# Where the stationary blocks of the expert matmuls begin, modulo 256 bytes

## The reference

```python
D_MODEL = 1024; N_EXPERTS = 32; TOP_K = 4; D_FF = D_MODEL
h = x + mix @ w_out
hn = rmsnorm(h, g_ffn_norm)
logits = (hn @ w_router).astype(jnp.float32) + b_router
top_v, top_e = lax.top_k(logits, TOP_K)
gates = jax.nn.softmax(top_v, axis=-1)
# for every block of rows that belongs to expert e:
h = xb @ w_gate_up[e] + b_gate_up[e]
gate = jnp.minimum(h[:, 0::2], SWIGLU_LIMIT)
up = jnp.clip(h[:, 1::2], -SWIGLU_LIMIT, SWIGLU_LIMIT)
glu = gate * jax.nn.sigmoid(gate * SWIGLU_ALPHA)
out = ((up + 1.0) * glu) @ w_down[e] + b_down[e]
y = h + sum over the 4 experts of gate * out
```

## Time and profile before

| | |
|---|---|
| median of 3 runs | 1380.27 us (1379.94 to 1383.11) |
| the profiled execution, its own time | 1378.44 us |
| its span, first to last instruction | 1376.7 us |
| PE busy | 1347.8 us, 98% of the span |
| DVE busy | 1208.2 us, 88% |
| ACT busy | 1090.7 us, 79% |
| mean granted TensorE clock | 0.993 of full speed |
| HBM | 340 GB/s over the span |

### The profile page before, as it was taken

One profiled execution on the slowest core, in us unless ns is written; L12 is line 12 of the kernel. 1 busy time (PEld: TensorE's weight loads), 2 busy tenths in 40 slices (PEclk: granted clock), 3 DMA queues, 4 the chain that ended last, 5 costly groups with the idle time before them and its releaser, 6 DMA issues.

```text
span 1376.7 us, 19701 instructions
## 1 busy us (share of the span) xinstructions
PE 1347.8 (98%) x6762; PEld 997.0 (72%) x6762; DVE 1208.2 (88%) x1092; ACT 1090.7 (79%) x1149; POOL 993.9 (72%) x431
## 2 busy tenths in 40 slices
PE   8999999999999999999999999999999999999995
PEld 5988655667777777777777777777777777777773
DVE  5466555899999999999999999999999999999996
ACT  5354413788889888888888888888888888888885
POOL 2122212266699999999999898898888888989843
PEclk9999998999999999999999999999999999999998
DMA  9521271999999999999999999999999999999984
GB/s 354 192 67 67 94 275 70 354 395 371 368 351 376 369 378 383 386 383 388 372 388 395 368 390 371 385 374 383 381 391 375 383 386 379 385 377 386 382 313 151
DMA packets 51802, 458.99 MB, mean 333 GB/s; under 512 B 11449, under 2 KB 15515, under 8 KB 26121
## 3 DMA queue, kind: packets, MB, share of 16 engines
q1 hardware_dynamic: 40089, 438.33, 81.1%
q0 software_dynamic: 10000, 18.19, 6.0%
q10 hardware_dynamic: 1648, 1.65, 0.4%
HBM read 446.62 MB, written 22.08 MB: 340 GB/s over the span
## 4 chain that ended last, share of the span: by engine, by line
PE 70%; DVE 6%; POOL 3%; issue 2%; DMA 1%; ACT 1%; POOLq 0%; ACTq 0%; DVEq 0%
PE psum L2376 22%; PE psum L2375 22%; PE psum L2374 22%; DVE low L1693 4%; PE psum L2358 1%; PE psum L2369 1%; DMA area<-hn_tbl,idx_i 1%; POOL brow L671 1%; POOL slot_tbl L724 1%; PE psum L1913 1%; POOL small L813 0%; DVE area L1775 0%; DVE area L1778 0%; DVE area L1768 0%; DVE area_r L1757 0%
## 5 line engine op out<-in xcount | busy, mean ns | idle before, releaser
L1693 DVE TENSOR_TENSOR low<-raw,high 128x2048 fp32r<-128x2048 f32 x384 | 872.8, 2304 | 32.9 <-ACT high L1101 32.8
L1101 ACT CAST high<-raw 128x2048 fp32r<-128x2048 f32 x384 | 727.4, 1913 | 20.2 <-PE psum L2376 17.1
L2374 PE MATMUL psum<-high,area_r 128*104 128x512 f32 x1536 | 606.3, 395 | 3.2 <-DVE area_r L1757 1.5
L2376 PE MATMUL psum<-low,area_r 128*104 128x512 f32 x1536 | 602.1, 392 | 0.0
L2375 PE MATMUL psum<-high,area_r 128*104 128x512 f32 x1536 | 599.7, 390 | 0.0
L671 POOL PARTITION_BROADCAST brow<-brow x192 | 325.4, 1773 | 45.8 <-DMA brow<-in_biases 45.4
L2374 PEld LDWEIGHTS psum<-high,area_r 128*104 128x104 f32 x1536 | 257.8, 168 | 93.3 <-DVE low L1693 2.1
L2376 PEld LDWEIGHTS psum<-low,area_r 128*104 128x104 f32 x1536 | 257.0, 167 | 93.7
L2375 PEld LDWEIGHTS psum<-high,area_r 128*104 128x104 f32 x1536 | 258.2, 168 | 88.5
L668 POOL COPY arrived<-cst 1x1 f32 x60 | 227.6, 3793 | 15.1 <-DMA brow<-in_biases 14.8
L740 POOL DMA_INDIRECT area<-hn_tbl,idx_i x32 | 162.8, 5088 | 79.6 <-DVE idx_i L1660 40.5
(11 more groups left out here) (269 smaller groups left out, 1150.3 us busy)
## 6 DMA issues: line engine op xcount, KB each, us to landing
raw<-in_w_gate_up SPq DMA_DIRECT2D x128, 2048.0 KB, 12.9
raw<-in_w_down SPq DMA_DIRECT2D x64, 2048.0 KB, 13.2
ring<-in_w_in SPq DMA_DIRECT2D x7, 1024.0 KB, 15.2
ring<-in_x_prompt SPq DMA_DIRECT2D x8, 512.0 KB, 9.9
ring<-in_w_out SPq DMA_DIRECT2D x7, 512.0 KB, 4.5
ring<-in_w_mem_kv SPq DMA_DIRECT2D x2, 1024.0 KB, 9.2
ring<-in_mem_kT SPq DMA_DIRECT2D x1, 2048.0 KB, 8.8
ring<-in_cache_mem_v SPq DMA_DIRECT2D x1, 2048.0 KB, 8.2
```

The costliest lines, as they stand in the source:

```text
L1101: nc.scalar.copy(high_w(i), raw_w(t)).then_inc(sem("w_high"), 1)
L1693: v.tensor_tensor(low_w(t), raw_w(t), high_w(i), ALU.subtract).then_inc(sem("w_low"), 1)
L2374: mm(bank, high, wh, start=False, stop=False, skip_group_check=True)
L2376: return mm(bank, high, wl, start=False, stop=stop, skip_group_check=True)
```

## The change

Two constants, `XO` = 48 numbers (192 bytes) and `AO` = 24 numbers (96 bytes). The blocks `xH`, `xL` begin 192 bytes further, the blocks `aH`, `aL` 96 bytes further modulo 256 (they also move by whole multiples of 256). The blocks stay 512 bytes apart. What lies behind them (`gt`, `sg`, `up`, `yrow`, `hot`) moves by 512 bytes; `posm`, `gate`, `rv`, `rv_all` and the rest do not move, since a maximum with a fixed offset sets their start. No instruction is added, removed or moved on any engine: each engine's list is the same, with other addresses.

```diff
@@ -48,6 +48,7 @@
 
 CAP = 104
 XS, AS = 128, 128
+XO, AO = 48, 24
 EXTRA = 20
@@ -231,10 +232,10 @@
         xg = moe_buf([2, D])
-        xH, xL = (view(area_r, a[0] + i * KD * XS, [KD, XS])[:, :, 0:CAP] for i in range(2))
-        a[0] += 2 * KD * XS
-        aH, aL = (view(area_r, a[0] + i * KD * AS, [KD, AS])[:, :, 0:CAP] for i in range(2))
-        a[0] += 2 * KD * AS
+        xH, xL = (view(area_r, a[0] + XO + i * KD * XS, [KD, XS])[:, :, 0:CAP] for i in range(2))
+        a[0] += 2 * KD * XS + XO
+        aH, aL = (view(area_r, a[0] - XO + AO + i * KD * AS, [KD, AS])[:, :, 0:CAP] for i in range(2))
+        a[0] += 2 * KD * AS + 128 - XO
         gt = moe_buf([2, 512])
```

## The result

Median of 6 runs 1389.63 us (1387.55 to 1391.61), beside 1381.01 us of the kernel before in as many runs (1379.94 to 1383.71): ratio 1.0063, 95% interval 1.0049 to 1.0077. The forecast was no measurable change, 1379. The profiled execution took 1387.94 us with a span of 1386.1, 9.4 us more than before. Behind the edited constants every line number is one higher: the products are now L2375, L2376, L2377, the transposes L2359 and L2370.

A forecast was written before the change was run, and what follows sets the result against it. PE's expert matmul gaps were taken to bound the kernel. Rows at -1.5 us, all else at nothing, took the profiled 1378.44 to 1376.9 and the median 1380.27 to 1378.8, rounded to 1379; range 1365 to 1390.

The forecast's parts named there:

- What bounds the kernel: PE, busy 98% of the span; an expert's time is the sum of its matmuls' start-to-start gaps, 228.9 ns each.
- the second rival: Expert matmuls: offsets not a multiple of 256 create a clash; +6 ns on activation, +9.2 us, 1389.5; slower, chance 0.22.
- Buffers behind the blocks and writes: Buffers moved by 512 bytes, and ACT and DVE writes of split blocks at another remainder: cost nothing, covered by slack.
- The step that failed: Rows matmuls at difference 192, priced from `z_half`'s second half: -0.5 ns each, -1.5 us, bounds 0 and -3.1 us.
- the upper bound at 0: Rows matmuls: no loss expected, as `z_half`'s halves, at differences 0/128 and 192/64, had excesses of 12.9 and 12.4 ns.
- The text's last sentence: Sign of error: a dependence `z_half` hides, its matmuls being half as long and its halves averaging over two differences each.
- The activation at 0: 1536 activation matmuls at difference 96, between neighbours at 64, 112 and 128: no change, bounds -1.5 and +9.2 us.
- The neighbour that pointed the right way: L2456, 104 stationary and 512 moving at difference 112: 235 ns each, 1 to 11 ns more than 228.9.
- The first rival: Expert matmuls: reads clash at difference 0, the change parts them; 3.2 ns each, 1370.4 or 1365.5 us; faster, chance 0.31.
- The rules of the Trainium skill: Expert matmuls: isolated-gap formula 215.8 ns, 60 us less, about 1320; independent read ports, no placing matters, 1380.3.

The follow-up runs named there:

- pad_all: Kernel before with 192 unused bytes ahead of everything, so all operands shift and the difference stays 0: 1381.00 us, ratio 1.0005.
- moving_only: Kernel before with 64 bytes ahead of ring, stationary blocks keeping their remainder, moving operands shifted, difference 192: 1394.76 us, ratio 1.0111.
- narrow_64: Kernel before with the experts' stationary blocks cut from 104 to 64 columns: 1383.03 us in one run, beside 1379.33.
- both_192: Changed kernel with rows and activation blocks both at difference 192: 1395.62 us, ratio 1.0109.
- both_96: Changed kernel with rows and activation blocks both at difference 96: 1380.13 us, ratio 1.0009.
- rows_only: Changed kernel with rows at difference 192 and activation moved 256 bytes, so at difference 0: 1387.18 us, ratio 1.0054.

## Why the prediction was wrong

- **What bounds the kernel: right.** The time of an expert is the sum of its matmuls' gaps. Mean gap times count gives +10.0 us against the +9.4 in the span, and no wait appeared. The 1389.63 us lie just inside the range of 1365 to 1390, but only because the range took in most of the second rival: the forecast itself was no measurable change, under 4.1 us, and the kernel lost 8.6.
- **Buffers behind the blocks and writes, at nothing: right** as far as it shows. DVE and ACT kept their busy times, and `pad_all`, which moves everything, costs nothing measurable (1.0005).
- **The step that failed: "For the rows this is the nearest row by difference (192 is in the second half): I take -0.5 ns, 3072 x -0.5 = -1.5 us, bounds 0 and -3.1 us."** The term measured +3.08 ns, +9.5 us, outside both bounds and on the other side. The neighbour was nearest in difference but not in shape, and its mean hid a dependence that its single gaps show. On average `z_half` (128 stationary, 272 moving) hardly moves: 0.5 ns between its halves, and 0.4 between `moving_only`, which shifts part of its blocks against its moving operands (125.2), and all other kernels (125.6), while the mean gap of the 104 x 512 matmuls went from 227.5 to 233.0. But gap by gap, `z_half` in the kernel before runs from 118 to 136 ns. Timeline of PE there, four matmuls that follow by 136, 124 and 119 ns:

```profile
53.94 0.30 PE L1970 MATMUL psum<-xl,area_r 128*128 128x272 f32 x1
54.08 0.28 PE L1971 MATMUL psum<-area_r,low 128*128 128x272 f32 x1
54.20 0.28 PE L1969 MATMUL psum<-area_r 128*128 128x272 f32 x1
54.32 0.29 PE L1970 MATMUL psum<-xl,area_r 128*128 128x272 f32 x1
```

The changed kernel has 136, 124 and 119 at the same place. Compared one by one with the kernel before, the gaps of `z_half` differ by 0.5 to 1.2 ns on average in every kernel that leaves its differences alone, `pad_all` too (0.8), and by 3.1 ns in `moving_only`. So the argument by which I closed the upper bound at 0, that a dependence on the difference "should have shown more than 1 ns between its halves", was wrong: it does not show in a mean over 24 matmuls. The text's last sentence named this weakness and gave it no number.
- **The activation at 0, bounds -1.5 and +9.2 us: right in size** (+0.3 ns, +0.5 us), by luck. It is a mean of two levels, 231.6 in the long train and 226.8 in the train of 36.
- **The neighbour that pointed the right way** was L2456, the one other place with exactly this shape. I read it to two decimals, as 1 to 11 ns slower than the experts with 6 in the middle; in the trace its last four gaps are 234, 233, 231 and 230 ns, 232.0 on average, 3 slower. And I let it bear on the activation alone, since 112 is near 96. Carried to the rows, 3 ns would have given +9.2 us. That this is the result is partly chance, since the trains on the rows at 192 take 226.7 to 233.4.
- **The second rival was right in its direction**: a start difference other than 0 creates a clash that 0 avoids. It had the place wrong, 6 ns on the activation where it was 3 on the rows; that its 1389.5 equals the measured time is chance. Its mechanism, a load left behind by a faster read, isn't shown, and a shorter load did not shorten the gap (`narrow_64`).
- **The first rival was not absurd**: at 96 and at 240 trains do run 2.3 ns below the 228.9 of difference 0. But its price of 3.2 ns is reached nowhere, the best mean (at 240) wins 1.5, and in the changed kernel only the trains of 36 run faster than before (226.8 ns on the activation, 226.9 on the rows at their end).
- **The rules of the Trainium skill.** In "SBUF — State Buffer", under who interferes with whom, PE's two read ports are independent and it waits on no one. By that rule no placing could matter, and the runs disagree: `moving_only` and `both_192` make each matmul 4 ns slower by the operands' start difference alone. In "TensorE: Matmul & The Clock Gate", under back-to-back issue gap, the formula for an isolated matmul, N / 2.4 + 2.5 ns, gives an estimate of 215.8 for 512 columns; in these trains no placing tried came nearer than 226.7.

**Open:** where the 13.4 ns between 226.7 and the 213.3 of the columns go (the levels 226.7, 230.0 and 233.3 are 544, 552 and 560 periods of 2.4 GHz, and no run says why); why 240 is good and 248 not; what at a train's restart picks the level (one transpose more changes it, its phase wasn't controlled); why the first trains settle on other levels than the later ones (the first eight are interrupted by `info`, but the ninth of `both_96` isn't and is slow too).

## What to carry to other kernels

Price a placement from a matmul of the same shape and type, even if its address is farther off, and don't set a bound at zero from the mean of one that is half as long: look at its single gaps first. Where TensorE is the bound, read start-to-start gaps per unbroken train rather than a mean: here the start of stationary against moving modulo 256 was worth from -0.1% to +1.1% of the whole kernel, and moving both operands together was worth nothing measurable. A gain per matmul counts only where nothing else is due: 6.9 us of shorter gaps became 1.4.

## What the runs showed of the hardware that I had not expected

- An fp32r matmul of 104 stationary and 512 moving columns follows the last by 226.7 to 233.4 ns in its trains at the 2.4 GHz level, by the difference of the operands' starts modulo 256 (227.5 in the mean at 240, 229.0 at 0, 232.9 at 192), and not by where both lie (one shift of 192 bytes tried: 229.0).
- At some differences there are two steady levels (226.7 and 231.6 at 96; 226.7 and 233.3 at 240, and in `rows_only` at 192). An unbroken train keeps its level over up to 94 gaps while the difference stays, and a changed level can be carried on: the rows matmuls at 192 take 226.9 behind activation matmuls that run at 226.8, and 232.7 behind those of the long train, at 231.6.
- A level is the mean of a short cycle of gaps that repeats: 229, 230, 232, 228, 234 ns in the long trains at difference 248, 226, 227, 227 at 240.
- A stationary block of 64 columns loads in 134 ns instead of 168, and the gap is 230.0 instead of 229.0.
- In `z_half` single gaps lie 18 ns apart (118 to 136) while the mean stays at 125.6: a pattern that comes back in every kernel which keeps the operands' differences.
